# Reordered stick-breaking pairs: one GpSimd instruction per weight remainder, the transposes at the end of each step, another tile order in the last pair

## The reference, cut to what matters

```
logits   = q k^T * scale
log_keep = where(key < query, log_sigmoid(-logits), 0)
between  = reverse_cumsum(log_keep) - log_keep
weights  = where(key < query, exp(log_sigmoid(logits) + between), 0)
y        = weights @ v
```

## Time and profile before

| what | value |
|---|---|
| median of 3 runs | 1587.31 us (1585.12 to 1588.14) |
| profiled execution | 1585.96 us |
| its span | 1584.1 us |
| mean granted TensorE clock | 0.945 |

### The profile page before, as it was taken

One profiled execution on the slowest core, in us unless ns is written; L12 is line 12 of the kernel. 1 busy time (PEld: TensorE's weight loads), 2 busy tenths in 40 slices (PEclk: granted clock), 3 DMA queues, 4 the chain that ended last, 5 costly groups with the idle time before them and its releaser, 6 DMA issues. The chain is left out here.

```text
span 1584.1 us, 23483 instructions
## 1 busy us (share of the span) xinstructions
PE 1410.7 (89%) x7206; PEld 1159.0 (73%) x7206; DVE 1014.2 (64%) x1773; ACT 900.3 (57%) x1758; POOL 513.9 (32%) x479
## 2 busy tenths in 40 slices
PE   6889899989898998975989599999999999996898
PEld 3667777777777777764877487788878778884676
DVE  4647777778787868677628846565565656557415
ACT  4555656555565655555425547676676767666422
POOL 2025445354545344434204322222322222221214
PEclk8999999999999999996999799999999999996999
DMA  9012111112111111103014211001001000102014
GB/s 344 20 56 63 36 54 47 53 46 60 46 43 43 53 53 49 57 20 133 8 40 165 60 41 28 27 26 40 26 26 40 26 26 26 40 13 107 0 54 172
DMA packets 88590, 89.88 MB, mean 57 GB/s; under 512 B 3065, under 2 KB 68834, under 8 KB 88546
## 3 DMA queue, kind: packets, MB, share of 16 engines
q1 hardware_dynamic: 88256, 89.15, 17.7%
q10 hardware_dynamic: 290, 0.18, 0.1%
HBM read 80.92 MB, written 8.40 MB: 56 GB/s over the span
## 5 line engine op out<-in xcount | busy, mean ns | idle before, releaser
L716 PE MATMUL bank<-h_hi,w_hi 128*128 128x512 f32 x976 | 404.4, 414 | 31.8 <-POOL w_lo L685 20.8
L716 PE MATMUL bank<-h_lo,w_hi 128*128 128x512 f32 x976 | 398.8, 409 | 0.0
L716 PE MATMUL bank<-h_hi,w_lo 128*128 128x512 f32 x976 | 398.4, 408 | 0.0
L685 POOL TENSOR_TENSOR w_lo<-w_raw,w_hi 128x256 fp32r<-128x256 f32 x236 | 221.5, 968 | 313.0 <-ACT w_hi L677 313.0
L1437 POOL TENSOR_TENSOR sa<-sa,keep 128x640 f32<-128x640 f32 (+7 forms) x128 | 159.8, 1249 | 387.0 <-DVE keep L1309 387.0
L716 PEld LDWEIGHTS bank<-h_hi,w_hi 128*128 128x128 f32 x976 | 189.4, 194 | 65.9 <-issue 33.5
L1309 DVE TENSOR_TENSOR_SCAN keep<-keep 128x640 f32<-128x640 f32 (+7 forms) x128 | 206.7, 1615 | 31.1 <-ACT keep L1201 29.9
L716 PEld LDWEIGHTS bank<-h_hi,w_lo 128*128 128x128 f32 x976 | 190.2, 195 | 36.0
L716 PEld LDWEIGHTS bank<-h_lo,w_hi 128*128 128x128 f32 x976 | 189.6, 194 | 32.1
L1200 ACT ACTIVATE sa<-bank 128x512 f32<-128x512 f32 (+1 forms) x192 | 94.6, 493 | 95.2 <-PE bank L1096 57.0
L1213 ACT ACTIVATE wt_hi<-bank 128x512 fp32r<-128x512 f32 (+1 forms) x192 | 87.5, 492 | 102.0 <-PE bank L1110 99.0
(11 more groups left out here) (220 smaller groups left out, 2931.9 us busy)
## 6 DMA issues: line engine op xcount, KB each, us to landing
w_raw<-in_w_in_dram SPq DMA_DIRECT2D x63, 512.0 KB, 4.0
ada_slice<-in_w_ada_dram SPq DMA_DIRECT2D x64, 256.0 KB, 2.7
p_ada<-in_w_ada_dram SPq DMA_DIRECT2D x8, 1024.0 KB, 13.2
wo_raw<-in_w_out_dram SPq DMA_DIRECT2D x8, 1024.0 KB, 8.2
p_x<-in_x_dram SPq DMA_DIRECT2D x8, 512.0 KB, 8.0
o_x<-in_x_dram SPq DMA_DIRECT2D x8, 512.0 KB, 4.2
x_between<-o_res SPq DMA_DIRECT2D x8, 512.0 KB, 2.9
o_x<-x_between SPq DMA_DIRECT2D x8, 512.0 KB, 4.1
```

Source lines behind the costliest of these rows:

```text
L685: ins = self.nc.gpsimd.tensor_tensor(self.m["w_lo"][s][:, ks, :], self.m["w_raw"][s][:, ks, :], self.m["w_hi"][s][:, ks, :].bitcast(F32), ...
L716: mm = nc.tensor.matmul(self.bank[half][:, :], w[:, k, :], h[:, k, half * HALF:(half + 1) * HALF], start=(i == 0), stop=(i == GROUP - 1))
```

## The change

- `split_lo` is one instruction of 128x1024 in both layers. In the loop the high parts are made at the end of steps 1, 5, 9, 13 (`W_HI_AT`) and the remainders ahead of `weigh` in steps 2, 6, 10, 14 (`W_LO_AT`).
- `turn` stands behind the second part of the share. `turn_values` moves to step 4 (`VALUES`), a quarter of the share stands ahead of it and three quarters behind.
- The adaLN slices are summed in steps 5, 7, 8, 9, 11, 12, 13, 15; their matmuls (L1121) move from output group 5 (step 15) to group 6 (step 1 of the next pair). The q remainder and k remainder of the second head move from steps 2 and 3 to steps 0 and 1.
- Last pair: tiles in the order i = 6, 7, 6, 7, 4, 5, 4, 5, 2, 3, 2, 3, 0, 1, 0, 1, by pairs of one head and the other. z takes steps 0 to 3, with both halves feature block by feature block, so that `h_lo` comes free by quarters (`z_freed`) and `w_out` is loaded by quarters. Its parts are made in steps 2 to 5 (high) and 5 to 8 (low), the output projection starts in step 9, with token blocks 6, 7, 4, 5 first (`order`). The gates are made and turned in steps 14 to 16.

```diff
-    def split_lo(self, pool, pair, kind):
+    def split_lo(self, engine, pair, kind):
         s = kind % 2
-        pool.wait_ge(self.hi_done, done(4 * pair + kind))
-        for k in range(0, KT, 2):
-            ks = slice(k, k + 2)
-            ins = self.nc.gpsimd.tensor_tensor(self.m["w_lo"][s][:, ks, :], ...)
-        ins.then_inc(self.lo_done, 1)
+        engine.wait_ge(self.hi_done, done(4 * pair + kind))
+        engine.tensor_tensor(self.m["w_lo"][s][:, :, :], self.m["w_raw"][s][:, :, :],
+                             self.m["w_hi"][s][:, :, :].bitcast(F32), ALU.subtract).then_inc(self.lo_done, 1)
...
-            if n == 0:
-                pe.wait_ge(self.weights_hi_done, KT * self.layer + KT)
+            if n < 2 * KT and i % 2 == 0:
+                pe.wait_ge(self.weights_hi_done, KT * self.layer + k + 1)
             if n == 2 * KT:
                 pe.wait_ge(self.weights_lo_done, KT * self.layer + KT)
...
-    LAST = Order([(0, 0), (0, 1), (1, 0), (1, 1), (0, 2), (1, 2), (0, 3), (1, 3)])
+    LAST = Order([(0, 3), (1, 3), (0, 2), (1, 2), (0, 1), (1, 1), (0, 0), (1, 0)])
+    VALUES = LAG + 1
...
-    SPLITS = [1, END[1] + 2, END[3] + 2, min(END[5] + 2, TILES - 1)]
-    LAST_Z = shares(2 * GROUP, [1] * 3 + [0] * (STEPS - 3))
-    HI_AT = {1: (3,), 2: (4,), 3: (5,), TILES - 4: (0,), TILES - 3: (1,), TILES - 2: (2,)}
-    LO_AT = {2: (2,), 3: (3,), TILES - 3: (0,), TILES - 2: (1,)}
-    ADA_AT = {s: k for k, s in enumerate((1, 2, 4, 6, 8, 10, 11, 13))}
-    ADA_GROUP = 5
+    W_HI_AT, W_LO_AT = {1: 0, 5: 1, 9: 2, 13: 3}, {2: 0, 6: 1, 10: 2, 14: 3}
+    HI_OWN, HI_NEXT = {0: (4, 5)}, {8: 0, 11: 1, 12: 2, 15: 3}
+    LO_OWN, LO_NEXT = {0: 2, 1: 3}, {9: 0, 12: 1}
+    ADA_AT = {s: k for k, s in enumerate((5, 7, 8, 9, 11, 12, 13, 15))}
+    ADA_GROUP = 6
+    LAST_Z = shares(2 * GROUP, [1] * 4 + [0] * (STEPS - 4))
+    GATES_AT = 16
...
-    MULTIPLY = shares(AHEAD * 2 * GROUP, [0] * 12 + [1] * (STEPS - 12))
-    AHEAD_AT = [{10: (0, 1), 14: (2,), 16: (3,), STEPS - 1: (AHEAD,)}.get(s, ()) for s in range(STEPS)]
+    OUT_HI_AT = {2 + k // 2: (k, k + 1) for k in range(0, KT, 2)}
+    OUT_LO_AT = {5 + k // 2: (k, k + 1) for k in range(0, KT, 2)}
+    MULTIPLY = shares(AHEAD * 2 * GROUP, [0] * 9 + [1] * (STEPS - 9))
+    AHEAD_AT = [{8: (0,), 9: (1,), 13: (2,), 16: (3,), STEPS - 1: (AHEAD,)}.get(s, ()) for s in range(STEPS)]
...
                     if s < TILES:
                         score(p, s)
-                    if s != LAG:
-                        share(p, s, project, 0)
+                    share(p, s, project, 0)
+                    if s == VALUES:
+                        turn_values(p)
                     for q, g in groups(p, s, first):
                         values(q, g)
-                    if s == LAG:
-                        turn_values(p)
-                        share(p, s, project, 0)
-                        share(p, s, project, 1)
+                    share(p, s, project, 1)
                     for q, t in tiles(p, s, first):
                         turn(q, t)
-                    if s != LAG:
-                        share(p, s, project, 1)
```

More of the change, by code:

```diff
@@ L719, in multiply @@
                 mm.then_inc(self.group_done, 1)
+            elif freed and kind == 3 and half == 1 and part == MULS - 1 and k % 2:
+                mm.then_inc(freed, 1)
     def keep(self, engine, pair, kind, half, pack, bank=None):
@@ L1065, in _ @@
                 pair(p)
[L1066 to L1070, removed]
+            ada(PAIRS - 1, 0)
+            outp.load_weights(sp, w_out, lambda n: (z_freed, n + 1) if n + 1 < KT // 2
+                              else (proj.group_done, done(8 * PAIRS - 1)))
+            ada(PAIRS - 1, *range(1, KT))
             sp.wait_ge(gate_kept, 1)
@@ L1157, in share, with turn_gates @@
                 proj.multiply(pe, p + 1, max(f, z) - z, max(l, z) - z)
+            def turn_gates():
+                pe.wait_ge(chain, 4)
+                pe.wait_ge(y_done, done(GROUPS * PAIRS - 3))
+                nc.tensor.transpose(O[0:DEPTH * KT, 3 * P:4 * P], m["gate_col"][:, :],
+                                    m["ident"][:, :]).then_inc(gate_turned, 1)
             def pair(p, first, project):
@@ L1180, in _ @@
             pair(PAIRS - 1, False, False)
-            pe.wait_ge(chain, 4)
-            nc.tensor.transpose(T[0][0:DEPTH * KT, 0:P], m["gate_col"][:, :], m["ident"][:, :]).then_inc(gate_turned, 1)
         @block.scalar
@@ L1249, in keep_u @@
                 if kind == 2:
-                    act.wait_ge(turned, done(NB * (p - 1) + half))
+                    act.wait_ge(turned, done(NB * (p - 1) + LOOP.ch[0] + half))
                 proj.keep(act, p, kind, half, pack, bank)
@@ L1267, in pair @@
                         weights_hi(q, t)
-                    for n in HI_AT.get(s, ()):
-                        if n >= 3 and not first:
-                            pack_hi(p, n)
-                        if n < 3 and project:
-                            pack_hi(p + 1, n)
                     for half in (Z_AT if project else LAST_Z_AT)[s]:
@@ L1276, in pair @@
                         keep_u(p + 1, kind, half)
+                    for n in () if first else HI_OWN.get(s, ()):
+                        pack_hi(p, n)
+                    if project and s in HI_NEXT:
+                        pack_hi(p + 1, HI_NEXT[s])
+                    if project and s in W_HI_AT:
+                        proj.split_hi(act, p + 1, W_HI_AT[s])
                     for t, h in () if project else ahead(MULTIPLY)[s]:
                         outp.keep(act, t, h)
-                    for k in () if project else range(*OUT[s]):
+                    for k in () if project else OUT_HI_AT.get(s, ()):
                         outp.weights_hi(act, k)
```

152 lines of the change are left out of this document (85 added, 67 removed).

## The result

The changed kernel takes 1600.88 us (median of 4 runs, 1600.14 to 1601.6), the kernel before 1587.21 beside it: a ratio of 1.0088, 95% interval 1.007 to 1.0105. It is slower by 14 us, where 17.5 us less was forecast. The direction was wrong; the nearest case was rival C (1604).

The account below looks back on a forecast made before the run. TensorE, busy 89%, was taken to set the pace, losing 10.9 of 85.3 us per looped pair. Terms -3 + 1 + 0 - 11 - 3 - 1.5 = -17.5 gave 1569 us; forecast 1555 to 1582 (chance 0.45), whole range 1530 to 1604.

Parts of the forecast that it names:

- rival C: Loop: whole remainder on the port delays scans, TensorE waits four times, then half clock; pair 89.7, kernel 1604; chance 0.25.
- (a) to (e): Looped pair: TensorE's waits on late VectorE remainders in steps 3, 4, 7, 11 and 15, 9.5 us in sum.
- (b): Step 4: 1024-column scan and an add stand ahead of the remainder that frees v's bank; wait 1.3 us.
- most of it falls where TensorE would wait again anyway: I take 1.0 for all: Looped pair: half clock after three waits over 2.02 us, up to 1.7 us each, counted as 1.0 together.
- the bound of 3.4: Looped pair: clock loss in the upper bound, 3.4 us, with no overlap of instructions giving a pair of 89.7.
- The base of 74.4: Looped pair: TensorE's own work, 74.4 of 85.3 us, the other 10.9 being loss.
- the 17th matmul at 68: Last pair: w_out's low part ready for the 17th output matmul at 68 us, from VectorE's work and waits.
- The wait on the k remainder: Last pair, step 2: second head's k remainder, made at the end of step 1, wanted at once; wait 5.7 us.
- The -11: Last pair: wide tiles first and earlier output projection, 117 us to its end against 127.8, so -11.
- 1.5 us left of 4.7: Behind the last pair: TensorE's 4.64 us wait for gates and next block shrinks to 1.5, so -3.
- "-1.5" for earlier gates: At `project_out`: earlier gates bring the broadcast gate earlier, -1.5 us (0 to -3).
- The row that I said weighs most: Profile rows: SBUF-only VectorE instruction doesn't run beside GpSimd's; k remainder took 2.95 us, a scan 2.75.

Follow-up runs that it names:

- e3: Changed kernel with GpSimd's product `weigh` ahead of the whole weight remainder in steps 2, 6, 10 and 14: 1548.00 us, ratio 0.9746.
- e1: Changed kernel with GpSimd's weight remainder again in four pieces of 128x256, at its new place: 1558.35 us, ratio 0.9817.
- e9: Changed kernel with the projections' weight remainders on VectorE, none on GpSimd in the looped pairs: 1538.73 us, ratio 0.9688.
- e7: e6 with the transposes ahead of the second part of the share again, in all steps but 4: 1529.13 us, ratio 0.9634.
- e12: Changed kernel with all layer 0 weight remainders on VectorE, last pair's k remainder a step early, transposes in mid-step: 1521.50 us, ratio 0.9586.
- e6: Changed kernel with the edits of e3 and e4 together: 1539.21 us, ratio 0.9701.
- e4: Changed kernel with the last pair's k remainder of the second head one step earlier, end of step 0: 1594.00 us, ratio 1.0041.
- e8: e3 with the last pair's tile order, token-block order and output projection start (step 12) as before the change: 1545.64 us, ratio 0.9741.
- e5: Kernel before the change with only the weight remainder as one whole instruction, still behind `weigh`: 1607.26 us, ratio 1.0131.

## Why the prediction was wrong

The changed kernel takes 32 us more than forecast. By stages of the profiled execution that is 16.9 in the six looped pairs, 9.2 in the last pair up to its last output matmul, 2.6 in the tail and 1.9 behind it; the rest lies in the prologue and pair 0.

**The waits (a) to (e) were right.** Forecast 2.55, 1.3, 1.2, 2.05 and 2.4, 9.5 in sum; pair 3 shows 2.99, 0.26, 1.11, 2.15 and 2.61, 9.1. Only (b) was too high. They are of the engine and line named. The mean of the six pairs is 9.2.

**The step that failed: "most of it falls where TensorE would wait again anyway: I take 1.0 for all".** That is the half clock behind the waits. The window of pair 3 around the first wait:

```profile
371.80:379.30 7.50, 4.51 (x20) 3.71 (x19) 4.52 (x7) 1.26 (x3) 1.77 (x1) 0.77 0.00 0
```

TensorE had been idle 2.99 us, and projection matmuls then start 0.43 us apart instead of 0.23, at the lower of the two levels (1.2 GHz), until 379.2. The six pairs have 12 such stretches, one to three in a pair, and the pair's length goes with their number: 86.2 us with one (pair 3), 87.8 with two, 89.1 with three (pair 2). Less its waits, a pair takes 77.0, 78.2 and 80.1 us in the mean with one, two and three, so about 1.5 each and 3.0 in the mean pair, where I had put 1.0. The same wait is followed by one in one pair and by none in another; what decides that I can't say from these runs. The forecast even named the bound of 3.4 and then chose the low end.

**The base of 74.4 was 1.0 too low.** The mean pair is 87.6 = 9.2 of waits + 3.0 of clock + 75.4. Pairs without half clock and with the transposes last confirm it: less their waits, e3's take 75.7, e1's and e9's 75.3. With the transposes in mid-step it is 74.9 (e7) and 74.5 (e12), where the same kernels with the transposes last have 75.8 (e6) and 75.3 (e9). So transposes last cost TensorE itself 0.8 to 0.9 us a pair. I had moved them at no cost. Whether it is the order or the refill behind each wait I haven't separated. With the waits 0.3 lower, the pair is 84.9 + 2.0 + 1.0 - 0.3 = 87.6, as measured.

**The last pair: the start right, the rest not.** Output matmuls began 67.1 us in (forecast 64 to 70). But I had the 17th matmul at 68, and it started at 74.7. The first 16 and the values matmuls between them ran for two thirds at half clock:

```profile
764.90:775.20 10.30, 6.14 (x20) 4.75 (x19) 10.30 (x8) 2.57 (x5) 6.35 (x3) 0.50 0.17 51
```

TensorE had been idle for 5.53 and 2.25 us before the clock fell at 764.9, and for 4.16 more right ahead of the first output matmul. The output matmuls need the low part of y, and VectorE makes it only behind its own `w_out` remainder, which takes 3.37 us beside one of GpSimd's (1.21 where GpSimd makes none, e12). That is not the whole of it: e12 still waits 3.43 us there.

```profile
765.24 3.37 DVE L863 TENSOR_TENSOR wo_lo<-wo_raw,wo_hi 128x1024 fp32r<-128x1024 f32 x1
768.53 1.21 DVE L881 TENSOR_TENSOR o_ahead_lo<-y,o_ahead_hi 128x1024 fp32r<-128x1024 f32 x1
```

```profile
769.85 0.76 PE L903 MATMUL bank<-wo_hi,o_ahead_hi 128*128 128x512 f32 x1 [4.16 <-issue]
```

The remaining work took 51.5 for the 49 reckoned. That makes 126.2 instead of 117. The kernel before is no longer: I had 127.8, the end of a window, but by the idle time of 4.64 ahead of 817.76 its last output matmul ended at 813.1, 126.3 us into the pair. So up to there the change gains 0.1 us, and the stage's 2.1 are all in the tail. The wait on the k remainder was seen (5.7, measured 6.22), and e4 shows that it costs 6.9. The -11 was put down to the wide tiles in part: with the late keys the order gives nothing (e8), without them 5.6 us (e6 against e8).

**The tail: 4.10 idle instead of 1.5.** The gates were in time, as I had said. What is late is the split of the fifth token block, the first of `project_out`, behind TensorE's last matmul: ScalarE's high part 1.05, VectorE's remainder 1.23, and the two adds 0.44 and 0.43 behind it, in a chain:

```profile
833.08 0.66 PE L2178 MATMUL bank<-wo_hi,o_ahead_hi 128*128 128x512 f32 x1 [4.10 <-PEq L1065]
```

The forecast had 1.5 us left of 4.7; in the kernel before it is 6.2 from the last output matmul to 819.34, and 4.10 are left. "-1.5" for earlier gates: +0.4 measured. The broadcast gate is loaded at `project_out`'s start in either kernel, so nothing was to be had.

**The row that I said weighs most did.** A VectorE instruction that reads SBUF alone doesn't run beside one of GpSimd: 0.69 became 2.77, 0.74 became 2.96, 1.21 became 3.37. The Trainium skill, in SBUF — State Buffer, section SBUF: two separate sides, says that the engine that starts first holds the shared port pair for its whole instruction; these rows agree, but for the 2.96, where GpSimd had the port although VectorE's instruction is recorded 0.03 us earlier. What I missed is what it is worth: I compared the new schedule with the old one, and never asked what it would be with the long instruction elsewhere. With the remainders elsewhere the change gains 39 us (e3 against before) to 50 (e9); the place of one GpSimd instruction in four steps costs 53 us (e3 against the changed kernel). Of rivals, C had the place, the instruction and the pair (89.7, measured 87.6) nearly right; it got 0.25 for the reason "steps 12 and 3 lose their present waits", which the base already contained.

## What to carry to other kernels

A long GpSimd instruction costs what VectorE has due on SBUF at the moment when it starts, not its own length. Put it behind something that itself waits for VectorE's last SBUF instruction of the stretch, cut it into pieces, or give it to VectorE; look at VectorE's durations, not at its busy share, to see the loss. A late VectorE instruction can also hold up a load behind it on SyncE's queue, and through it a third engine (e5). Where waits of 2 to 3 us on TensorE are forecast, put a price on the half clock behind them. Here 18 waits of over 2 us in the six looped pairs stood beside 12 stretches of 1.5 us each; in e3, e6, e7 and e9 to e12, with no wait over 1.3 us, there was none.

## What the runs showed of the hardware

- Moving four instructions from GpSimd to VectorE left VectorE's recorded busy time as it was (63.24 and 63.28 us a pair): recorded busy time holds the time in which an instruction waits for the other engine.
- Four GpSimd pieces of 128x256 share with VectorE at the cost of GpSimd: 5.90 us where the whole one took 3.34 in the same step, waiting included, and VectorE lost 0.9 instead of 2.1.
- When both engines want SBUF at nearly the same time, either may be first. At 432.46 VectorE's sum started 0.03 us ahead of GpSimd's remainder, as recorded, and still ended 0.54 behind it; at 367.88 VectorE started 0.15 us ahead and took its usual 1.22.
- The same GpSimd instruction took 2.38 to 3.34 us in the loop, and VectorE's version of it 1.38 to 2.11 (e9).
- VectorE's remainders of the transposed weights, which read PSUM, take their 0.69 us for 128x512 beside GpSimd's work as well as alone. The VectorE instructions that grew in the changed kernel all read SBUF alone.
